# Norm, projection and head norms of a two-layer trunk as one pipeline over token tiles

## The reference

```
m  = (silu(c) @ mod_w[i] + mod_b[i]).reshape(nb_b, N_MOD, 1, d)
mc = (silu(c_ctx) @ mod_w[i] + mod_b[i]).reshape(N_MOD, d)
h  = rms_norm(x, norm1_g[i]) * (1.0 + m[:, 1]) + m[:, 0]
hc = rms_norm(xc, norm1_g[i]) * (1.0 + mc[1]) + mc[0]
p  = h @ w_in[i]
pc = hc @ (w_in[i] if update_ctx else w_in[i][:, :Q_OFF])
ckv = rms_norm(p[..., KV_OFF:KR_OFF], kv_a_norm_g)      # 128 wide
kv  = einsum('blr,rhe->blhe', ckv, w_ukv)               # 8 heads, 64 for k and 64 for v
k   = apply_rope(rms_norm(concat(k_nope, k_rope), k_norm_g))
cq  = rms_norm(p[..., Q_OFF:CONV_OFF], q_a_norm_g)      # 256 wide
q   = apply_rope(rms_norm(einsum('blr,rhe->blhe', cq, w_uq), q_norm_g))
```

## Time and profile before

| | us |
|---|---|
| median of three runs | 2565.8 (2565.45 to 2572.3) |
| the profiled execution | 2566.59 |
| its span, first to last instruction | 2564.5 |
| PE busy | 2222.2 (87%) |
| DVE busy | 887.6 (35%) |
| ACT busy | 651.0 (25%) |
| POOL busy | 176.8 (7%) |

### The profile page before, as it was taken

One profiled execution on the slowest core, in us unless ns is written; L12 is line 12 of the kernel. 1 busy time (PEld: TensorE's weight loads), 2 busy tenths in 40 slices (PEclk: granted clock), 3 DMA queues, 4 the chain that ended last, 5 costly groups with the idle time before them and its releaser, 6 DMA issues.

```text
span 2564.5 us, 26788 instructions
## 1 busy us (share of the span) xinstructions
PE 2222.2 (87%) x10625; PEld 1712.2 (67%) x10625; DVE 887.6 (35%) x1094; ACT 651.0 (25%) x1013; POOL 176.8 (7%) x281
## 2 busy tenths in 40 slices
PE   2767999999999999759999836799999999779994
PEld 0435688888888888437777624467788777567773
DVE  0455631232332532331111173653334453411113
ACT  0244531321121222211111133353322222211111
POOL 3030000000000000010110221100000000011101
PEclk6987999999999999969999959799999999879997
DMA  9601011221221313569999950102324343189995
GB/s 349 214 20 32 1 38 42 74 58 47 74 74 46 111 51 131 225 250 362 365 369 364 336 182 1 49 1 62 103 70 107 87 127 111 58 294 366 365 371 215
DMA packets 316092, 397.60 MB, mean 155 GB/s; under 512 B 10912, under 2 KB 271104, under 8 KB 308832
## 3 DMA queue, kind: packets, MB, share of 16 engines
q1 hardware_dynamic: 288256, 297.56, 36.4%
q0 software_dynamic: 15360, 53.64, 5.9%
q10 hardware_dynamic: 12384, 45.09, 4.4%
HBM read 359.45 MB, written 36.80 MB: 155 GB/s over the span
## 4 chain that ended last, share of the span: by engine, by line
PE 58%; DVE 6%; DMA 3%; issue 2%; ACT 2%; POOL 1%; POOLq 0%; ACTq 0%; DVEq 0%
PE ps L587 23%; PE ps L975 14%; PE ps L984 7%; PE ps L589 4%; PE ps L577 2%; PE ps L967 2%; DMA HTF<-in_mod_w 2%; PE ps L783 2%; PE ps L608 1%; DMA MGZ<-y_rows,slot_i 1%; PE ps L933 0%; PE ps L742 0%; PE ps L767 0%; PE ps L768 0%; PE ps L769 0%
## 5 line engine op out<-in xcount | busy, mean ns | idle before, releaser
L587 PE MATMUL ps<-HTH,WS 128*128 128x512 f32 x1664 | 579.6, 396 | 15.8 <-issue 7.3
L587 PEld LDWEIGHTS ps<-HTH,WS 128*128 128x128 f32 x1664 | 313.6, 188 | 89.3 <-issue 9.8
L587 PE MATMUL ps<-HTL,WS 128*128 128x512 f32 x832 | 327.9, 394 | 0.0
L975 PE MATMUL ps<-RING,MGZ 128*128 128x256 f32 x1216 | 276.3, 385 | 2.8 <-ACT MGZ L1342 2.8
L1508 DVE TENSOR_TENSOR WS<-RAWB,WS 128x1024 fp32r<-128x1024 f32 (+1 forms) x128 | 190.5, 1490 | 220.9 <-ACT WS L1152 220.5
L975 PEld LDWEIGHTS ps<-RING,MGZ 128*128 128x128 f32 x1216 | 232.8, 193 | 35.5 <-ACT MGZ L1342 3.9
L589 PE MATMUL ps<-HTH,WS 128*128 128x256 f32 x832 | 233.9, 281 | 0.0
L1152 ACT ACTIVATE WS<-RAWB 128x1024 fp32r<-128x1024 f32 (+1 forms) x128 | 162.6, 1272 | 270.7 <-PE ps L589 138.2
L587 PE MATMUL ps<-BRH,WS 128*128 128x512 f32 x512 | 181.7, 394 | 6.4 <-DVE BRL L1671 3.6
L587 PEld LDWEIGHTS ps<-HTL,WS 128*128 128x128 f32 x832 | 156.9, 189 | 36.2 <-issue 1.0
L984 PE MATMUL ps<-RING,MGZ 128*128 128x512 f32 x392 | 176.4, 593 | 0.5 <-ACT MGZ L1346 0.5
(11 more groups left out here) (300 smaller groups left out, 3188.7 us busy)
## 6 DMA issues: line engine op xcount, KB each, us to landing
RING<-in_moe_w SPq DMA_DIRECT2D x125, 1024.0 KB, 7.5
RAWB<-in_w_in SPq DMA_DIRECT2D x112, 512.0 KB, 4.0
HTF<-in_moe_w SPq DMA_DIRECT2D x25, 1024.0 KB, 7.4
y_rows<-MGZ ACTq DMA_DIRECT2D x50, 512.0 KB, 6.9
MGZ<-in_mod_w SPq DMA_DIRECT2D x24, 1024.0 KB, 6.1
HTF<-in_mod_w SPq DMA_DIRECT2D x24, 1024.0 KB, 8.0
RAWB<-in_w_branch SPq DMA_DIRECT2D x64, 256.0 KB, 4.5
RAWB<-in_w_o SPq DMA_DIRECT2D x16, 512.0 KB, 4.1
```

Source lines behind the costliest of these rows:

```text
L587: last = mm(psb(pair)[:, 0:SEQ], a[:, k0 + k, :], b[:, k, 0:SEQ], start=go, stop=end)
L975: last = mm(psb(1)[:, o:o + FF], xgT[j][:, k, :], slot3(s, KD)[:, k, :], start=(k == 0), stop=(k == KD - 1))
```

## The change

1. Shift and scale of the first norm no longer go through DRAM. The rows of turn 0, with norm1_g as a third row beside them, are transposed on PE (four 128 x 128 blocks) and copied by DVE to columns in T: shift, gain and (1 + scale) x gain for each vector and block (`mod_columns`). The norm itself only multiplies by the root. After the transposes, when a channel is a partition, ACT applies scale and shift in place in PSUM, eight activations of 128 columns for a tile (`modulated`).
2. Norm, projection and heads form one loop over tiles on each engine: PE in iteration i projects tile i, transposes the latents of i - 1 and the rows of i + 1, and multiplies the heads of i - 1; ACT and DVE reach from the norm of tile i + 2 to the head norms of tile i - 2. The latent norms go tile by tile. One pair of PSUM banks takes the transposes, banks 2 and 3 the projections in turn.
3. In layer 0, SP loads eight slabs first, then the first weights, and then turns 1 and 2 as 32 half slabs of 512 KB through a ring of three. PE takes 6, 10, 5, 5 and 6 of them at the ends of iterations 0 to 4. x is asked for after five slabs instead of three, and each tile of it has its own semaphore.
4. Between the layers the combine of the experts moves into the same loop, POOL adds to x, and there are two pairs of gather buffers instead of three, in layer 1 too. kvq is split ahead of the loop.
5. Rope's table, the ones beside the values and two rows of the spatial gate are loaded or written at other places on POOL.

The core of the diff:

```diff
 MSLOTS, TURNS, MSLABS = 3, N_MOD * D // SLAB, KD * (N_MOD * D // SLAB)
+MOD_SLABS = [(0, 0, k, 0, SLAB) for k in range(KD)] + \
+            [(0, u, k, half, SLAB // 2) for u in range(1, TURNS) for half in range(2) for k in range(KD)] + \
+            [(1, u, k, 0, SLAB) for u in range(TURNS) for k in range(KD)]
...
-            for n in range(MSLABS // 2):
-                mod_load(0, n)
+            for g in range(MOD_DONE[0, 0]):
+                mod_load(g)
...
-                    if l == 0 and r == RAWS - 1:
-                        for n in range(MSLABS // 2, MSLABS):
-                            mod_load(0, n)
+                    if l == 0 and r == FIRST:
+                        for g in range(MOD_DONE[0, 0], MOD_DONE[0, TURNS - 1]):
+                            mod_load(g)
...
+                rows_up(0)
+                for i in range(AT + 1):
+                    if i < AT:
+                        project(i)
+                    if i >= 1:
+                        latent_T(i - 1)
+                    if i + 1 < AT:
+                        rows_up(i + 1)
+                    if i >= 1:
+                        heads_up(i - 1)
+                    if l == 0:
+                        mod_turns(min(MOD_DONE[0, 0] + (6, 16, 21, 26, 32)[min(i, 4)], MOD_DONE[0, TURNS - 1]))
...
-            act.wait_ge(S("mod_used"), 3)
+            act.wait_ge(S("mod_used"), 5)
...
+                def modulated(t):
+
+                    v = 0 if t < LT else 1
+                    act.wait_ge(S("h_tr"), at("h_tr", l, t + 1))
+                    act.wait_ge(S("hcol"), l + 1)
+                    for k in range(KD):
+                        o = psb(0)[:, k * P:(k + 1) * P]
+                        last = act_f(o, o, ACT.Identity, scale=scale1[:, v, k:k + 1], bias=shift1[:, v, k:k + 1])
+                    last.then_inc(S("h_aff"), 1)
...
+                for i in range(-3, AT + 2):
+                    if l and i + 3 < AT:
+                        weighted(i + 3)
+                    if 0 <= i + 2 < AT:
+                        squares(i + 2)
+                    if 0 <= i - 2 < AT:
+                        head_roots(i - 2)
+                    if 0 <= i + 2 < AT:
+                        root(i + 2)
+                    if 0 <= i - 1 < AT:
+                        latent_rows(i - 1)
+                    if 0 <= i < AT:
+                        latent_squares(i)
+                    if 0 <= i + 1 < AT:
+                        modulated(i + 1)
+                    if 0 <= i < AT:
+                        latent_roots(i)
+                    if 0 <= i + 1 < AT:
+                        modulated_hi(i + 1)
+                    if 0 <= i - 1 < AT:
+                        evacuate(i - 1)
...
+                for i in range(-3, AT + 2):
+                    if l == 0 and i in (2, 5):
+                        mod_rows_out(0, 1 if i == 2 else 2, bank(7))
+                    if l and i + 3 < AT:
+                        summed(i + 3)
+                    if 0 <= i - 2 < AT:
+                        head_squares(i - 2)
+                    if 0 <= i + 2 < AT:
+                        mean_eps(i + 2)
+                    if 0 <= i - 2 < AT:
+                        head_norms(i - 2)
+                    if 0 <= i < AT:
+                        latent_eps(i)
+                    if 0 <= i + 2 < AT:
+                        normed(i + 2)
+                    if 0 <= i + 1 < AT:
+                        modulated_lo(i + 1)
+                    if 0 <= i < AT:
+                        small_norms(i)
...
+                fetch(0)
+                fetch(1)
+                for t in range(NT):
+                    if t + 2 < NT:
+                        fetch(t + 2)
+                    if l + 1 < DEPTH:
+                        pool.wait_ge(S("y_g"), at("y_g", l, t + 1))
+                        pool.tensor_tensor(x_t[:, t, :], x_t[:, t, :], ytmp[t % 2], ALU.add).then_inc(S("x_new"), 1)
```

More of the change, by code:

```diff
@@ L408, in trunk @@
         raw_full = [S(f"raw_full{s}") for s in range(RAWS)]
+        x_in = [S(f"x_in{t}") for t in range(AT)]
+        x_out = [S(f"x_out{t}") for t in range(AT)]
         def split_no(l, s):
@@ new lines, in latent_T, with heads_up @@
+                def latent_T(t):
+                    pe.wait_ge(S("cn"), at("cn", l, t + 1))
+                    for j in range(3 if t < NT else 1):
+                        last = pe.transpose(bank(2 + t % 2)[:, j * P:(j + 1) * P], cn[t % 2][:, j * P:(j + 1) * P], ident[:, :])
+                    last.then_inc(S("cn_tr"), 1)
+                wukv, wuq = raw_slab(3, D), raw_slab(4, 2 * H * QK).rearrange("p (k n) -> p k n", k=2)
+                def heads_up(t):
+                    n0 = up_items(l, t)
+                    if t == 0:
+                        pe.wait_ge(raw_full[0], full_no[l, 3])
+                        pe.wait_ge(raw_full[1], full_no[l, 4])
+                    pe.wait_ge(S("cnT"), at("cnT", l, t + 1))
+                    if t < NT:
+                        for j in range(2):
+                            if j and t:
+                                pe.wait_ge(S("up_sb"), at("up_sb", l, n0 - 2))
+                            for k in range(2):
+                                last = mm(bank(6 if j else 2 + t % 2)[:, 0:384], cnT[t % 2][:, (1 + k) * P:(2 + k) * P],
+                                          wuq[:, k, j * 384:(j + 1) * 384], start=(k == 0), stop=(k == 1))
+                            last.then_inc(S("up_ps"), 1)
+                    for j in range(2):
+                        if t:
+                            pe.wait_ge(S("up_sb"), at("up_sb", l, n0 - 1 + j))
+                        mm(bank(4 + j), cnT[t % 2][:, 0:P], wukv[:, j * 512:(j + 1) * 512], start=True, stop=True)\
+                            .then_inc(S("up_ps"), 1)
@@ L1080, in _, with weighted @@
+                act.dma_start(x_t[:, t, :], src).then_inc(x_in[t], 16)
             for l in range(DEPTH):
                 NT = tiles(l)
[L1082 to L1085 removed]
+                def weighted(t):
+                    act.wait_ge(S(f"yg{t % 2}"), at(f"yg{t % 2}", l - 1, 32 * (t // 2 + 1)))
+                    if t >= 2:
+                        act.wait_ge(S("x_new"), at("x_new", l - 1, t - 1))
+                    act_f(ytmp[t % 2], yg[t % 2][0], ACT.Copy, scale=gw[0][:, t:t + 1]).then_inc(S("y_w0"), 1)
@@ new lines, in squares, with root @@
+                def squares(t):
+                    if l:
+                        act.wait_ge(S("x_new"), at("x_new", l - 1, t + 1))
+                        act.dma_start(x_spill[t * P:(t + 1) * P, :], x_t[:, t, :]).then_inc(x_out[t], 16)
+                    else:
+                        act.wait_ge(x_in[t], 16)
+                    act_f(htok[t % 2], x_t[:, t, :], ACT.Square, scale=D ** -0.5, accum_out=st[:, t:t + 1]).then_inc(S("n1_sq"), 1)
+                def root(t):
+                    act.wait_ge(S("n1_eps"), at("n1_eps", l, t + 1))
+                    act_f(srt[:, t:t + 1], rst[:, t:t + 1], ACT.Sqrt).then_inc(S("n1_rt"), 1)
```

500 lines of the change are left out of this document (228 added, 272 removed).

## The result

Four runs of the changed kernel took 2530.9 to 2544.7 us, median 2536.6; the kernel before took 2565.5 to 2572.3 beside them, median 2567.3. The ratio is 0.988, with a 95% interval from 0.985 to 0.991: faster, by 30.7 us between the medians, where 67 had been forecast. The profiled execution took 2530.9 us with a span of 2529.2, 35.3 less than the span before. Measured again with the last experiments, the changed kernel's median was 2533.8 (ratio 0.987 [0.985, 0.988]).

The account below looks back on a forecast made before the run. Stretches each limited by another engine stand one behind the other, after a memory-bound start; a pipeline over tiles overlaps them. 2566.6 - 31 (layer 0) - 39 (layer 1) + 3.5 (last combine) = 2500 us, range 2470 to 2545.

Parts of the forecast that it names:

- First projection of layer 0: Start of layer 0: fewer loads and no DRAM round trip let the first projection start at 50 us, against 94.
- The bounds: Start of layer 0: first projection at 46 us if bytes land as early as possible, 60 if weights come last.
- 38 us for them and 40.5 for their rounding: Start of layer 0: kvq weights landed by 38 us and rounded, ahead of the norm on ScalarE and VectorE, by 40.5.
- Groups of 6, 10, 5, 5, 6 then stand on TensorE for 5.6, 12.8, 5.1, 5.1, 5.6: Layer 0 pipeline: time TensorE spends per group of half slabs, at 0.52 us matmul each and 4.1 per ring round.
- Iterations without feeding: Pipeline over tiles: two loops run beside each other, 11.2 us per iteration, 12.4 with one VectorE and GpSimd disturbance.
- The tail of layer 0: Layer 0, sixth projection at 137 us to end of head norms: 31 us of serial steps plus 2 for the clock.
- ScalarE first finishes the second tile's square: Start of layer 1: a wait counted before the first tile's modulation, which ends at 1495.5 us; first projection at 1498.
- Tail: Last combine of layer 1: two gather buffers instead of three make the fourth gather later, 3.5 us lost.
- (b): Layer 0 feeding: half slabs land no faster than whole ones, 6.1 us, seven ring rounds by 2.5 more: 2517 us, chance 0.12.
- (a): Layer 1: GpSimd's adds under two-input VectorE work stretch to 7.5 us, delaying the first projection and VectorE: 2518, chance 0.08.
- (c): Both pipelines: TensorE drops to 1.2 GHz in every gap, 19 us per iteration: 2568, chance 0.04; in half: 2534, chance 0.14.
- (d): Both pipelines: the loops close in series through fixed orders on ScalarE and VectorE, 21 us per iteration: 2574, chance 0.06.

Follow-up runs that it names:

- the last two versions: Changed kernel plus half slabs in four blocks, spread feeding, first norm before kvq rounding, reordered ScalarE and VectorE, three gather buffers; two feeding tables: 2496.7 and 2497.3 us.
- The order alone: Against the changed kernel, first tile modulated and rounded before the second's squares, root and norm, and head squares before the combine: 2534.1 us, ratio 0.988.

## Why the prediction was wrong in size

The profiled execution was to gain 66.6 us and its span gained 35.3. Of the 31 us between them 23 are layer 0 (8.4 won of 31) and 5.5 layer 1 (33.5 of 39); 4.5 are the stretches in between, for which the sum had nothing, and the tail gave 1 back. The second trace of the changed kernel puts 27 into layer 0.

- **First projection of layer 0**: 50 forecast, 56.4 and 57.3 measured. The bounds (46 to 60) held. A smaller step failed here, "38 us for them and 40.5 for their rounding": the kvq pieces landed until 43.5 and were rounded at 45.5 on ScalarE and 47.2 on VectorE. From there the rest took about the 10 us forecast, though the modulation was 2.87 and not 2.2 at most. That the norm need not stand behind them at all shows in the last two versions, which also round the first tile earlier: 50.7 and 52.4.
- **Feeding in layer 0**: this is the main step that failed, "Groups of 6, 10, 5, 5, 6 then stand on TensorE for 5.6, 12.8, 5.1, 5.1, 5.6". They stood for 9.2, 18.7, 9.0, 9.0, 8.9. Of the 21 us too many, 17.4 are the price of a half slab, 1.03 and more at the lower clock for my 0.52 (34.0 against 16.6), and 3.5 are waits (21.1 against 17.6). I had halved the time of a whole slab. But its matmuls go to four groups of 32 output partitions and run side by side; a half has only two of the four, and lasts as long. The four blocks of 256, at 0.61 at the upper clock in that trace, show it, and so do the three half slabs in 1.89 above. Sending half slabs for the two pairs of groups by turns would follow from this; it was not run. The landing, 3.6 from the spill of x, was 4.9. That neither is repaired alone is the other lesson: cheaper matmuls gave 4 to 8 us at the sixth projection, where the waits stayed and the clock fell; taking the waits away gave 19 to 23.
- **Iterations without feeding**: 11.2 to 12.4 forecast, 11.4 to 13.5 measured, mean 12.3. Right within about 1 us. The tail of layer 0 was 33 by the forecast, and 30.6 and 31.0 measured.
- **Layer 1**: 32 us from the last expert to the first projection, 61 to the sixth, 24 to the end; measured 36.4, 64.9, 21.4. "ScalarE first finishes the second tile's square" was right, but that square waits for the second tile's combine, GpSimd's two gathers and its add, and the root behind it for VectorE; I had counted none of that. The order alone gave 3.9 of these 4 back. The 4 us too many in the iterations are a net: 13.6 and 16.0 where 11.2 and 12.4 were forecast, and 2.4 less in the last two. I put the 16.0 down to the first head norm, which waits behind the combine of the sixth tile; moving the head sums ahead gave 0.4, and the rows above show that the wait moved with them: the combine, for which the forecast's iteration has no term, and GpSimd's add still stand in its chain.
- **Tail**: 3.5 forecast, 3.8 measured with two buffers against three.
- **Rivals**: (b) named the right place and 2517, for another reason: half slabs did land faster than whole ones, 4.9 against 6.1. (a) falls as it was put, with adds of 7.5 us: they took 2.35, and there was no gain where VectorE does them. It is VectorE that waits, 2.5 us in the combine of 3.74. (c) shows in part: the clock was 0.86 to 0.91 in the iterations, and 0.83 only where the matmuls were made cheaper and the waits stayed. That its 2534, for half of the gaps, lies beside the measured 2537 is chance: it has layer 1 lose 13 us against the forecast, where 5.5 were lost. (d) falls by the run without feeding.

With the feeding spread and cut as I had priced it, with the first norm ahead, the order and the third buffer, the time is 2497. That this is near the forecast of 2500 confirms no step of it: the forecast had 34.2 us of feeding, 17.6 of them waits, where this version has 22.0, and it counted two gather buffers where this one has three.

## What to carry to other kernels

Side work that waits for loads belongs in small portions between the steps of a loop on the engine that carries the loop, no more at a time than the ring holds; one group at the end of each iteration shows every load's latency. Price a cut instruction by what ran beside it: halves of a thing that ran in parallel cost the whole. In a pipeline over fixed orders, ask of each first tile what stands ahead of it on each engine, and what that in turn waits for.

## What the runs showed of the hardware

- Matmuls with two output rows: four of 512 columns into four partition groups 1.04 us together, two into two groups 1.03, four of 256 columns into four groups 0.61, all at the upper clock. The Trainium skill, TensorEngine Tiling (Array Packing), section Tiling Modes, has the array split by columns into four tiles of 128 x 32 that work independently; these rows agree.
- A VectorE combine that meets a GpSimd add ends a fixed time after it, as if it waited the add out. Combines of 1.28 alone took 3.74 (1484.63 to 1488.37, the add ended at 1487.28) and 1.69 (1479.43 to 1481.12, the add ended at 1480.03): both end 1.09 us after the add. The add keeps its 2.35. The Trainium skill, SBUF — State Buffer, section Who interferes with whom, calls the port pair that the two share an exclusive lock whose loser blocks for the whole instruction. The rows agree in that. By the same section whoever issues first gets the pair. At 1484.63 VectorE's row starts 0.3 us ahead of the add and still waits, so the start in a row does not tell who has it.
- The clock fell in one trace when side work got cheaper and the waits stayed: with 34.0 to 37.6 us of feeding matmuls and 19 to 22 of waits in the five iterations 0.86 to 0.91 was granted, with 21.5 us and 24.6 of waits 0.83, and the other matmuls went from 375 to 460 ns. Cheaper side work alone does not do it: with 17.4 us and 8.6 of waits 0.96 was granted, with 29.8 and 4.1 also 0.96, and with nearly no feeding 0.92.
